# Segment sums of a Mamba stage: from full-height matmuls to differences of running sums on 32-row groups

## The chip, the cores and the metric

The kernel is one program on one core of a Trainium2 chip. The metric is the device time of one execution in microseconds (us). Three runs of the kernel before are shown, and one execution was profiled.

## The reference

A decoder trunk of two layers on 256 tokens of width 1024, in float32. Each layer adds to `h` first a combined mixer of three head groups (forgetting attention, HGRN2, Mamba-2), then cross-attention to 256 memory tokens, then a SwiGLU (layer 0) or a top-2-of-8 mixture of experts (layer 1). The part that matters here is the Mamba-2 group, 8 heads in 2 groups:

```python
a_dt = dt * a                       # one value per token and head, never positive
a_cum = jnp.cumsum(a_dt, axis=-1)
seg = a_cum[..., :, None] - a_cum[..., None, :]
lmat = masked_exp(seg, _causal_mask(ln))
cb = jnp.einsum('bclgn,bcsgn->bgcls', cc, bc)
y_diag = jnp.einsum('bgecls,bcsgep->bclgep', cb[:, :, None] * lmat, xc)
...
y = (y_diag + y_off) + d_skip * xs
```

`seg` for tokens l and s is the sum of `a_dt` over the tokens after s and up to l. The kernel takes the whole sequence as two tiles of 128 tokens, so each head has three blocks of 128 x 128: tile 0 to itself, tile 0 to tile 1, tile 1 to itself.

## The kernel before

Five engines run their own instruction streams, written out by hand, and meet by semaphores. Weights come in chunks of up to 1 MB (SyncE's queue, a ring of 4 slots, `RING`). Of each chunk ScalarE makes a "high" part (`whi`, L594, a ring of 3, `HRING`) and VectorE the remainder, the "low" (`wlo`, L1556). TensorE multiplies high by high, high by low and low by high (L1039 to L1041). `split_to(n)` makes highs or lows up to chunk n, `after(name)` up to three chunks past the projection `name`. A chunk takes TensorE 48 matmuls of 256 columns or 24 of 512.

Projections are interleaved with the heads' work, in this order in each layer: gates, `hq_hf`, `fq_fk`, `fv_hi`, the forgetting attention, `xbc0`, `xbc1` (inputs of the Mamba convolution), nine levels of the HGRN2 heads (L1180, L1185; 64-row matmuls of two alternating row groups) with `z` between them, then `xk0`, and the Mamba stage:

1. half of `xk0`, the outputs of the HGRN2 heads (L1198 to L1200, PSUM bank 7), the other half of `xk0`;
2. the products of B and C (L1208, L1209) and the transposes of x (L1212), in banks 4 to 7. ScalarE copies the transposes to `xs` (L802), VectorE masks the products into `CBs` (L1854);
3. round 0, heads 0 to 3: the segment sums in banks 4 to 7. ScalarE takes their exponential into `Mm` (L806), VectorE multiplies by `CBs` (L1872);
4. half of `xk1`, then round 1, heads 4 to 7, in the same banks, then the other half of `xk1`;
5. the heads' products with x (L1233 to L1235), which wait for both products of `Mm` (`m2_m`) and signal `m2_y`.

A round makes three full-height fp32 matmuls for each head. `ALm` holds the token's value at every column below it, and `ABm` the value at all columns (VectorE expands both ahead of the stage, L1841 and L1843):

```python
nc.tensor.matmul(b[:, 0:2 * P], ALm[:, 0, hd, :], upto_ones, start=True, stop=False)
nc.tensor.matmul(b[:, P:2 * P], ABm[:, hd, :], upto, start=False, stop=True)
mm = nc.tensor.matmul(b[:, 2 * P:3 * P], ALm[:, 1, hd, :], upto, start=True, stop=True)
```

Round 0 waits for `m2_a` (the expansions), `m2_cb` (L1854) and `m2_xs` (L802).

Of the kernel before, what the change touches and what calls it, by code (L numbers as in the profile page):

```python
# [38 lines left out]
EPS = 1e-6  # L39
FLOOR = 1e-30  # L40
# [49 lines left out]
for _name, _w in (("ident", P), ("minus_half", 20), ("neg", P), ("upto", P), ("ones", P), ("after", P), ("m2mask", 3 * P),  # L90
                  ("before", P), ("restart", 2 * S), ("iota", P), ("pair", NE)):
    CCOL[_name] = (_n, _n + _w)
    _n += _w
# [3 lines left out]
def constants():  # L97
# [4 lines left out]
    one = np.ones((P, P), np.float32)  # L102
    restart = np.broadcast_to((np.arange(2 * S) % 64 != 0).astype(np.float32), (P, 2 * S))
    parts = [np.eye(P, dtype=np.float32), np.full((P, 20), -0.5), (upto - np.eye(P)) * NEG, upto, one, (r[:, None] > r[None, :]) * 1.0,
             upto, one, upto, upto - np.eye(P), restart, np.broadcast_to(np.arange(P), (P, P)),
             (r[:, None] % NE == np.arange(NE)[None, :]) & (r[:, None] < 2 * NE)]
# [14 lines left out]
def build(nc, x, mem, par, con, lvl, lin_w, ffn_w, out):  # L121
# [31 lines left out]
    with ExitStack() as ctx:  # L153
# [86 lines left out]
        Mm = carve(8736, M2_H, 3 * P)  # L240
# [3 lines left out]
        ALm = carve(14368, NT, M2_H, P)  # L244
        ABm = carve(2560, M2_H, P)
# [124 lines left out]
        m2_a = sem("m2_a")  # L370
        m2_seg = sem("m2_seg")
        m2_e = sem("m2_e")
# [76 lines left out]
        def bank(name, layer):  # L449
            return 2 * (GI[name, layer] % 2)  # L450
# [5 lines left out]
        def _(sp):  # L456
# [125 lines left out]
        def _(act):  # L582
# [88 lines left out]
            for layer in range(DEPTH):  # L671
# [74 lines left out]
                ins.then_inc(fox_p, 1)  # L746
                def take_xbc(i):
# [48 lines left out]

                act.wait_ge(conv_ready, layer + 1)
                nc.scalar.activation(xcv, xcv, ACT.Silu).then_inc(xcv_ready, 1)
                take("z", layer, (zs, 0, 512, ACT.Silu, 1.0, None))
                split_to(last_chunk(layer, "xk0") + 2)  # L800
                act.wait_ge(m2_t, layer + 1)
                nc.scalar.activation(xs, pb[:, 6:8, :], ACT.Copy).then_inc(m2_xs, 1)  # L802
                take("xk0", layer, (tiles(kX[:, 0:4, :]), 0, 512, ACT.Copy, 1.0, None))
                for r in range(2):
                    act.wait_ge(m2_seg, 2 * layer + r + 1)
                    nc.scalar.activation(Mm[:, 4 * r:4 * r + 4, :], pb[:, 4:8, 0:3 * P], ACT.Exp).then_inc(m2_e, 1)  # L806
                    if r == 1:
                        split_to(chunk0(layer, "xk1") + HRING)
# [195 lines left out]
        def _(pe):  # L1004
# [96 lines left out]
            for layer in range(DEPTH):  # L1101
# [50 lines left out]
                project("xbc1", layer, X, (0,))  # L1152
                pe.wait_ge(fox_ptc, layer + 1)
# [37 lines left out]
                project("xk0", layer, M, (0,))  # L1191
                pe.wait_ge(hg_sel, (layer + 1) * (MASKED + 1))
                pe.wait_ge(hg_wide, (layer + 1) * len(WIDE))
                for hd in range(HG_H):
                    v = vtok[:, :, 256 + hd * DH:256 + (hd + 1) * DH]
                    at = 4 * (hd % 2) + 2 * (hd // 2)
                    o = pb[:, 7, :].rearrange("p (t h d) -> p t h d", t=NT, h=HG_H)
# [7 lines left out]
                pe.wait_ge(hg_ok, layer + 1)  # L1205
# [8 lines left out]
                pe.wait_ge(m2_a, layer + 1)  # L1214
                pe.wait_ge(m2_cb, layer + 1)
                pe.wait_ge(m2_xs, layer + 1)
                for rnd in range(2):
                    if rnd:
                        project("xk1", layer, M, (0,))
                        pe.wait_ge(m2_e, 2 * layer + 1)  # L1220
                    for i in range(4):
                        hd = 4 * rnd + i
                        b = pb[:, 4 + i, :]
                        nc.tensor.matmul(b[:, 0:2 * P], ALm[:, 0, hd, :], upto_ones, start=True, stop=False)  # L1224
                        nc.tensor.matmul(b[:, P:2 * P], ABm[:, hd, :], upto, start=False, stop=True)  # L1225
                        mm = nc.tensor.matmul(b[:, 2 * P:3 * P], ALm[:, 1, hd, :], upto, start=True, stop=True)  # L1226
                    mm.then_inc(m2_seg, 1)
                project("xk1", layer, M, (1,))
                pe.wait_ge(m2_m, 2 * layer + 2)
                for hd in range(M2_H):  # L1230
                    xh = xcd[:, :, hd * DH:(hd + 1) * DH]
                    o = slice(hd * DH, (hd + 1) * DH)
                    nc.tensor.matmul(pb[:, 4, o], Mm[:, hd, 0:P], xh[:, 0, :], start=True, stop=True)  # L1233
                    nc.tensor.matmul(pb[:, 5, o], Mm[:, hd, P:2 * P], xh[:, 0, :], start=True, stop=False)  # L1234
                    mm = nc.tensor.matmul(pb[:, 5, o], Mm[:, hd, 2 * P:3 * P], xh[:, 1, :], start=False, stop=True)  # L1235
# [303 lines left out]
        def _(dve):  # L1539
# [119 lines left out]
            for layer in range(DEPTH):  # L1659
# [120 lines left out]
                V.tensor_reduce(nmax[:, 4:8], pb[:, 4:8, P:3 * P], AX.X, ALU.max, negate=True).then_inc(fox_max, 1)  # L1780
                after("fv_hi", layer)
# [482 lines left out]
```

## Time and profile before

| | |
|---|---|
| time, median of 3 runs | 1516.91 us (1515.53 to 1518.87) |
| the profiled execution: time | 1518.24 us |
| the profiled execution: span from first to last instruction | 1515.9 us |
| mean granted TensorE clock | 0.995 of full |
| TensorE, VectorE, ScalarE busy | 1481.3, 1174.5, 940.8 us |
| Mamba stage in the span | about 117 to 154 us (layer 0) and 563 to 599 us (layer 1) |

In a timeline the first number is the start in us from the begin of the span, the second the length. A matmul's length holds its way through the array, and successive ones overlap: what one costs is the distance to the next start. An fp32 matmul leaves two records (x2), one of fp32r or a transpose one. The number in brackets at the end is the engine's idle time before the row, and behind the arrow the instruction that ended it.

### The profile page before, as it was taken

What the parts mean: (1) busy time and instruction counts of PE and PEld (TensorE: products, weight loads), DVE (VectorE), ACT (ScalarE), POOL (GpSimd) and SP (SyncE); (2) the same over time, 40 slices, a digit from 0 to 9 for tenths busy, and PEclk for the clock granted to TensorE, in tenths of its full rate; (3) what the DMA queues carried; (4) which work ended last, traced back from release to release, by engine and by line L of the source; (5) the groups of instructions that cost most, each with busy time, mean ns of one, the idle gap of its engine ahead of it and who ended that gap; (6) DMA issues with size and microseconds to landing.
All of it is one profiled execution on the core that took longest, in us unless ns stands there. A gap on an engine that the chain in (4) does not pass through costs nothing.

```text
span 1515.9 us, 21517 instructions
## 1 busy us (share of the span) xinstructions
PE 1481.3 (98%) x8411; PEld 1288.7 (85%) x8411; DVE 1174.5 (77%) x1140; ACT 940.8 (62%) x959; POOL 52.2 (3%) x58
## 2 busy tenths in 40 slices
PE   8999999999999999999999999999999999999996
PEld 7989898999889989897788888888888888888885
DVE  6886655555437886646998988989989899898995
ACT  6645344444337653454677778777787777777774
POOL 0031000000000031000000000000000000000000
PEclk9999999999999999999999999999999999999998
DMA  8433443454546432544699999999999998999993
GB/s 308 142 136 103 150 165 127 151 191 174 191 153 228 148 113 84 194 140 167 228 360 383 347 353 356 351 377 359 343 358 348 378 363 339 362 354 373 362 362 128
DMA packets 54478, 388.41 MB, mean 256 GB/s; under 512 B 6000, under 2 KB 6256, under 8 KB 8176
## 3 DMA queue, kind: packets, MB, share of 16 engines
q1 hardware_dynamic: 53840, 384.98, 67.8%
q10 hardware_dynamic: 544, 2.10, 0.4%
q8 instruction: 69, 1.13, 0.3%
q14 instruction: 25, 0.20, 0.0%
HBM read 386.00 MB, written 1.05 MB: 255 GB/s over the span
## 4 chain that ended last, share of the span: by engine, by line
issue 53%; PE 44%; DVE 2%; DMA 0%; ACT 0%; POOL 0%; POOLq 0%; DVEq 0%
PE pb L1039 12%; PE pb L1041 12%; PE pb L1040 12%; PE pb L1180 1%; PE pb L1258 1%; PE pb L1278 1%; PE pb L1020 1%; DVE xTl L1605 0%; PE pb L1224 0%; DMA h<-in_x 0%; PE pb L1268 0%; PE pb L1235 0%; PE pb L1226 0%; PE pb L1234 0%; PE pb L1225 0%
## 5 line engine op out<-in xcount | busy, mean ns | idle before, releaser
L2121 DVE TENSOR_TENSOR wlo<-raw,whi 128x2048 fp32r<-128x2048 f32 x175 | 400.3, 2291 | 47.7 <-ACT whi L941 45.9
L941 ACT ACTIVATE whi<-raw 128x2048 fp32r<-128x2048 f32 x175 | 335.6, 1920 | 132.0 <-PE pb L1041 132.0
L1556 DVE TENSOR_TENSOR wlo<-raw,whi 128x2048 fp32r<-128x2048 f32 (+1 forms) x101 | 225.7, 2246 | 133.2 <-ACT whi L594 132.7
L1039 PE MATMUL pb<-whi,mTh 128*128 128x512 f32 x768 | 305.2, 397 | 1.6 <-DVE wlo L2121 1.6
L1041 PE MATMUL pb<-whi,mTl 128*128 128x512 f32 x768 | 300.1, 391 | 0.0
L594 ACT ACTIVATE whi<-raw 128x2048 fp32r<-128x2048 f32 (+1 forms) x101 | 189.9, 1884 | 176.9 <-PE pb L1041 166.2
L1039 PE MATMUL pb<-xTh,whi 128*128 128x256 f32 x736 | 210.2, 286 | 2.0 <-DVE xTl L1593 1.2
L2121 DVE TENSOR_TENSOR kvXr<-kvX,whi 128x2048 fp32r<-128x2048 f32 x86 | 196.7, 2291 | 19.3 <-ACT whi L941 17.8
L1040 PE MATMUL pb<-xTl,whi 128*128 128x256 f32 x736 | 208.2, 283 | 0.0
L1041 PE MATMUL pb<-xTh,wlo 128*128 128x256 f32 x736 | 208.2, 283 | 0.0
L1040 PE MATMUL pb<-wlo,mTh 128*128 128x512 f32 x528 | 205.6, 389 | 0.0
L941 ACT ACTIVATE whi<-kvX 128x2048 fp32r<-128x2048 f32 x86 | 165.2, 1920 | 57.7 <-PE pb L1041 57.5
L1039 PEld LDWEIGHTS pb<-whi,mTh 128*128 128x128 f32 x768 | 144.2, 188 | 31.1 <-DVE wlo L2121 2.9
L1041 PEld LDWEIGHTS pb<-whi,mTl 128*128 128x128 f32 x768 | 144.1, 188 | 31.1
L1039 PEld LDWEIGHTS pb<-xTh,whi 128*128 128x128 f32 x736 | 141.1, 192 | 3.7 <-issue 2.1
L1040 PEld LDWEIGHTS pb<-xTl,whi 128*128 128x128 f32 x736 | 141.2, 192 | 0.1
L1041 PEld LDWEIGHTS pb<-xTh,wlo 128*128 128x128 f32 x736 | 141.1, 192 | 0.0
L1039 PE MATMUL pb<-whi,xhTh 128*128 128x512 f32 x352 | 138.5, 393 | 0.3 <-DVE wlo L2121 0.3
L1041 PE MATMUL pb<-whi,xhTl 128*128 128x512 f32 x352 | 137.1, 390 | 0.0
L1040 PEld LDWEIGHTS pb<-wlo,mTh 128*128 128x128 f32 x528 | 99.3, 188 | 19.8
L1040 PE MATMUL pb<-kvXr,mTh 128*128 128x512 f32 x240 | 93.5, 389 | 0.0
L1040 PE MATMUL pb<-wlo,xhTh 128*128 128x512 f32 x240 | 93.4, 389 | 0.0
(334 smaller groups left out, 2223.2 us busy)
## 6 DMA issues: line engine op xcount, KB each, us to landing
raw<-in_ffn_w SPq DMA_DIRECT2D x209, 1024.0 KB, 4.8
kvX<-in_ffn_w SPq DMA_DIRECT2D x88, 1024.0 KB, 4.9
raw<-in_lin_w SPq DMA_DIRECT2D x64, 1024.0 KB, 4.8
raw<-in_lin_w SPq DMA_DIRECT2D x4, 536.0 KB, 5.6
arena<-in_mem ACTq DMA_DIRECT2D x2, 1024.0 KB, 8.2
h<-in_x SPq DMA_DIRECT2D x1, 1024.0 KB, 5.0
out<-xn SPq DMA_DIRECT2D x2, 512.0 KB, 3.1
consts<-in_con SPq DMA_DIRECT2D x1, 836.0 KB, 14.0
```

The lines of the kernel that those rows point to most:

```text
L594: nc.scalar.activation(whi[:, m % HRING, c], raw[:, m % RING, c], ACT.Copy).then_inc(hi_ready, 1)
L941: nc.scalar.activation(whi[:, (MOE0 + c) % HRING, :], xraw_slots[c % XRING], ACT.Copy).then_inc(hi_ready, 1)
L1020: mm = nc.tensor.transpose(pb[:, turn_bank(no, b), i * S + t * P:i * S + (t + 1) * P], xn[:, t, k * P:(k + 1) * P], ident)
L1039: nc.tensor.matmul(o, lh, rh, start=first, stop=False)
L1040: nc.tensor.matmul(o, lh, rl, start=False, stop=False)
L1041: return nc.tensor.matmul(o, ll, rh, start=False, stop=last)
L1180: mm = nc.tensor.matmul(pb[:, b + hd % 2, i * P:(i + 1) * P], K[r, o + t * P:o + (t + 1) * P], Q[r, o + t * P:o + (t + 1) * P], start=True ...
L1258: mm = nc.tensor.matmul(pb[:, 4 + hd, t * S:(t + 1) * S], qX[:, 2 * hd + k, t * P:(t + 1) * P], kX[:, 2 * hd + k, :], start=(k == 0), stop ...
L1278: mm = nc.tensor.matmul(pb[:, 4 + hd, k * S:(k + 1) * S], vX[:, m, c:c + P], PTx[:, hd, m, :], start=(m == 0), stop=(m == 1))
L1556: V.tensor_tensor(wlo[:, m % RING, c], raw[:, m % RING, c], whi[:, m % HRING, c].bitcast(F32), ALU.subtract).then_inc(lo_ready, 1)
L2121: V.tensor_tensor(xlo_slots[c % XRING], xraw_slots[c % XRING], whi[:, (MOE0 + c) % HRING, :].bitcast(F32), ALU.subtract).then_inc(lo_ready, 1)
```

## The change

The segment sums are made as differences of running sums.

- In the forgetting-attention stage VectorE makes for each head and tile a value rounded to a coarse step (`COARSE`) and the rest, in four columns of each 32-column group of `Wm`. Four matmuls of TensorE, for both rounds, give their running sums over the tokens in bank 7 (`m2_c`), four rows for each of four heads of a round, on rows 0, 32, 64 and 96. ScalarE scales and shifts them by a table of 0, 1 and -1 (`units`) into `Qm` and `Km` (`m2_rows`), ahead of its work for `xbc0`.
- A round is then eight matmuls on 32 rows each: for i = 0 to 3, rows 32i to 32i+31, one of 256 columns into bank 4+i, and then four of 128 columns.
- Since rounded differences can come out above zero, VectorE takes the minimum with 0 of the two blocks of a tile with itself, in place in PSUM (`nonpositive`), before ScalarE's exponential.
- Round 0 moves ahead of the outputs of the HGRN2 heads, which go to the second bank of `z` and wait for `z`'s evacuation. Round 1 moves behind the first half of `xk1`. `Mm` becomes two tiles.
- ScalarE evacuates `z` ahead of `xcv`, takes exponential 0 ahead of `xk0`, then `xk0`, `xs`, exponential 1.
- VectorE: the expansions go; squares of the heads ahead of `CBs`; product 0 and `xcd` ahead of the low that `after("xk0")` makes; `ytmp` and the low of `xk1`'s ring behind the heads' normalisation.
- SyncE requests the level masks (`lmask`, 512 KB, first used by the HGRN2 levels) behind chunk 7 instead of chunk 3 of layer 0.

```diff
@@ SyncE
                     load(chunk0(layer, PROJ[0][0]) + c, lin_w[layer * LIN_CHUNKS + c])
+                    if layer == 0 and c == RING + 3:
+                        sp.dma_start(lmask[:, :, :].rearrange("p a b -> p (a b)"), lvl).then_inc(masks_in, 16)
                     if layer == 0 and c == RING - 1:
                         sp.dma_start(consts[:, early:], con[:, early:]).then_inc(tables_in, 16)
                         sp.dma_start(params[:, columns:], par[:, columns:]).then_inc(tables_in, 16)
-                        sp.dma_start(lmask[:, :, :].rearrange("p a b -> p (a b)"), lvl).then_inc(masks_in, 16)
@@ ScalarE, behind the attention's exponentials
+                act.wait_ge(m2_c, layer + 1)
+                units = [const("units")[:, i:i + 1] for i in range(4)]
+                sums = pb[:, 7, :].rearrange("p (r s) -> p r s", r=2)
+                nc.scalar.activation(Qm, sums, ACT.Identity, scale=units[0], bias=units[1])
+                nc.scalar.activation(Km, sums, ACT.Identity, scale=units[2], bias=units[3]).then_inc(m2_rows, 1)
@@ ScalarE, the stage
+                projected(act, "z", layer)
+                b = bank("z", layer)
+                nc.scalar.activation(zs, pb[:, b:b + 2, 0:512], ACT.Silu).then_inc(lin_act, 1)
                 act.wait_ge(conv_ready, layer + 1)
                 nc.scalar.activation(xcv, xcv, ACT.Silu).then_inc(xcv_ready, 1)
-                take("z", layer, (zs, 0, 512, ACT.Silu, 1.0, None))
-                split_to(last_chunk(layer, "xk0") + 2)
+                after("z", layer)
+                def decays(r):
+                    act.wait_ge(m2_neg, 2 * layer + r + 1)
+                    nc.scalar.activation(Mm[r], pb[:, 4:8, 0:3 * P], ACT.Exp).then_inc(m2_e, 1)
+                decays(0)
+                take("xk0", layer, (tiles(kX[:, 0:4, :]), 0, 512, ACT.Copy, 1.0, None))
                 act.wait_ge(m2_t, layer + 1)
                 nc.scalar.activation(xs, pb[:, 6:8, :], ACT.Copy).then_inc(m2_xs, 1)
-                take("xk0", layer, (tiles(kX[:, 0:4, :]), 0, 512, ACT.Copy, 1.0, None))
-                for r in range(2):
-                    act.wait_ge(m2_seg, 2 * layer + r + 1)
-                    nc.scalar.activation(Mm[:, 4 * r:4 * r + 4, :], pb[:, 4:8, 0:3 * P], ACT.Exp).then_inc(m2_e, 1)
-                    if r == 1:
-                        split_to(chunk0(layer, "xk1") + HRING)
+                decays(1)
+                split_to(chunk0(layer, "xk1") + HRING)
@@ TensorE, behind the transposes of the attention weights
+                pe.wait_ge(m2_w, layer + 1)
+                for rnd in range(2):
+                    o = pb[:, 7, rnd * S:(rnd + 1) * S]
+                    nc.tensor.matmul(o[:, 0:P], Wm[:, 0, rnd, :], const("after"), start=True, stop=True)
+                    mm = nc.tensor.matmul(o[:, P:S], Wm[:, 1, rnd, :], upto, start=True, stop=True)
+                mm.then_inc(m2_c, 1)
@@ TensorE, the stage
                 project("xk0", layer, M, (0,))
+                def segments(rnd):
+                    for i in range(4):
+                        r = slice(32 * i, 32 * i + 32)
+                        nc.tensor.matmul(pb[:, 4 + i, 0:2 * P], Km[r, rnd, 0:P], Qm[r, rnd, :], start=True, stop=True)
+                    for i in range(4):
+                        r = slice(32 * i, 32 * i + 32)
+                        mm = nc.tensor.matmul(pb[:, 4 + i, 2 * P:3 * P], Km[r, rnd, P:S], Qm[r, rnd, P:S], start=True,
+                                              stop=True)
+                    mm.then_inc(m2_seg, 1)
                 pe.wait_ge(hg_sel, (layer + 1) * (MASKED + 1))
                 pe.wait_ge(hg_wide, (layer + 1) * len(WIDE))
+                segments(0)
+                pe.wait_ge(lin_act, evac_count(("z", layer)))
...
                 mm.then_inc(m2_t, 1)
-                pe.wait_ge(m2_a, layer + 1)
+                project("xk1", layer, M, (0,))
                 pe.wait_ge(m2_cb, layer + 1)
                 pe.wait_ge(m2_xs, layer + 1)
-                for rnd in range(2):
...
+                segments(1)
+                pe.wait_ge(hg_ok, layer + 1)
                 project("xk1", layer, M, (1,))
                 pe.wait_ge(m2_m, 2 * layer + 2)
@@ VectorE, behind the maxima of the attention
+                for t in range(NT):
+                    ins = V.tensor_scalar(Z12[:, t, 4:12], A12[:, t, 4:12], 2.0 * t - 1.0, COARSE, ALU.mult, ALU.add)
+                link(ins)
+                for t in range(NT):
+                    at = Wm[:, t, :, :].rearrange("p r (i x) -> p r i x", x=32)
+                    V.tensor_scalar(at[:, :, :, 0:2], pairs(Z12[:, t, 4:12]), -COARSE, None, ALU.add)
+                    ins = V.scalar_tensor_tensor(out=at[:, :, :, 2:4], in0=pairs(Z12[:, t, 4:12]), scalar=-COARSE,
+                                                 in1=pairs(A12[:, t, 4:12]), op0=ALU.add,
+                                                 op1=ALU.subtract if t else ALU.add)
+                ins.then_inc(m2_w, 1)
@@ VectorE, the stage
-                V.tensor_copy(ABm, bc(A12[:, 1, 4:12], P))
-                for t in range(NT):
-                    ins = V.tensor_tensor(ALm[:, t, :, :], const("after").unsqueeze(1).to_broadcast([P, M2_H, P]),
-                                          bc(A12[:, t, 4:12], P), ALU.mult)
-                ins.then_inc(m2_a, 1)
+                def nonpositive(rnd):
+                    dve.wait_ge(m2_seg, 2 * layer + rnd + 1)
+                    own = pb[:, 4:8, 0:3 * P].rearrange("p b (i s) -> p b i s", i=3)[:, :, 0:3:2, :]
+                    V.tensor_scalar(own, own, 0.0, None, ALU.min).then_inc(m2_neg, 1)
+                nonpositive(0)
...
+                split_to(last_chunk(layer, "xk0") + 2)
                 dve.wait_ge(m2_t, layer + 1)
                 V.tensor_tensor(CBs, pb[:, 4:6, 0:3 * P], const("m2mask")...
+                decayed(0)
+                dve.wait_ge(m2_xs, layer + 1)
+                for t in range(NT):
+                    V.tensor_tensor(by_heads(xcd, t), by_heads(xs, t), bc(SP12[:, t, 4:12], DH), ALU.mult)
                 after("xk0", layer)
+                nonpositive(1)
+                decayed(1)
                 root()
```

## Rows read from the trace of the kernel before

**Rows 1.** The page: busy time by engine, and the chain that ended last, by engine.

```profile
PE 1481.3 (98%) x8411; PEld 1288.7 (85%) x8411; DVE 1174.5 (77%) x1140; ACT 940.8 (62%) x959; POOL 52.2 (3%) x58
...
issue 53%; PE 44%; DVE 2%; DMA 0%; ACT 0%; POOL 0%; POOLq 0%; DVEq 0%
```

**Rows 2.** TensorE's timeline, layer 0: start, length, line, operation, count, idle before.

```profile
117.61 0.33 PE L1198 MATMUL pb<-arena 128*128 128x64 f32 x2
...
129.59 0.67 PE L1224 MATMUL pb<-consts,arena 128*128 128x256 f32 x2 [1.21 <-ACT arena L802]
...
130.54 0.60 PE L1224 MATMUL pb<-consts,arena 128*128 128x256 f32 x2
130.98 0.38 PE L1225 MATMUL pb<-consts,arena 128*128 128x128 f32 x2
131.20 0.39 PE L1226 MATMUL pb<-consts,arena 128*128 128x128 f32 x2
...
133.10 0.36 PE L1039 MATMUL pb<-mTh,whi 128*128 128x256 f32 x1
...
138.92 0.59 PE L1224 MATMUL pb<-consts,arena 128*128 128x256 f32 x2
...
142.21 0.39 PE L1226 MATMUL pb<-consts,arena 128*128 128x128 f32 x2
142.35 0.36 PE L1039 MATMUL pb<-mTh,whi 128*128 128x256 f32 x1
...
148.18 0.33 PE L1233 MATMUL pb<-arena 128*128 128x64 f32 x2
```

**Rows 3.** TensorE's timeline, the same stage in layer 1.

```profile
575.13 0.67 PE L1224 MATMUL pb<-consts,arena 128*128 128x256 f32 x2 [1.21 <-ACT arena L802]
...
593.72 0.33 PE L1233 MATMUL pb<-arena 128*128 128x64 f32 x2
```

**Rows 4.** TensorE's timeline, the first two levels of the second heads, layer 0.

```profile
88.11 2.16 PE L1180 MATMUL pb<-arena 64*128 64x128 f32 x32
90.19 0.50 PE L1039 MATMUL pb<-whi,xTh 128*128 128x512 f32 x1
90.53 0.39 PE L1040 MATMUL pb<-wlo,xTh 128*128 128x512 f32 x1
90.76 0.39 PE L1041 MATMUL pb<-whi,xTl 128*128 128x512 f32 x1
```

**Rows 5.** ScalarE's timeline, layer 0.

```profile
90.09 1.07 ACT L751 ACTIVATE arena<-pb 128x512 f32<-128x512 f32 x2
...
113.59 1.28 ACT L798 ACT_TABLE_LOAD   x1
...
142.63 1.46 ACT L806 ACTIVATE arena<-pb 128x1536 f32<-128x1536 f32 x1 [7.71 <-PE pb L1226]
```

**Rows 6.** VectorE's timeline, layer 0.

```profile
28.51 2.23 DVE L1556 TENSOR_TENSOR wlo<-raw,whi 128x2048 fp32r<-128x2048 f32 x1
...
68.27 1.76 DVE L1789 COPY arena<-pb 128x1536 f32<-128x1536 f32 x1 [0.92 <-PE pb L1147]
...
70.17 2.29 DVE L1556 TENSOR_TENSOR wlo<-raw,whi 128x2048 fp32r<-128x2048 f32 x1
...
128.43 0.96 DVE L1854 TENSOR_TENSOR arena<-pb,consts 128x768 f32<-128x768 f32 x1 [5.10 <-PE pb L1212]
...
144.12 1.76 DVE L1872 TENSOR_TENSOR arena<-arena 128x1536 f32<-128x1536 f32 x1 [3.66 <-ACT arena L806]
...
153.68 1.22 DVE L1885 TENSOR_TENSOR xn<-arena,pb 128x1024 f32<-128x1024 f32 x1 [3.53 <-PE pb L1235]
```

**Rows 7.** TensorE's timeline around its first weight wait, layer 0.

```profile
30.58 0.28 PE L1041 MATMUL pb<-xTh,wlo 128*128 128x256 f32 x1
30.89 0.35 PE L1039 MATMUL pb<-xTh,whi 128*128 128x256 f32 x1
```

**Rows 8.** Line L1224: weight loads, length in ns (lowest, median, highest).

```profile
L1224 PEld LDWEIGHTS pb<-consts,arena x32: 186/192/192, 129.6 to 587.1; 128*128 128x128 f32 x32
```

More of the change, by code:

```diff
@@ L39 @@
 EPS = 1e-6
+COARSE = 3.0 * 2.0 ** 10
 FLOOR = 1e-30
@@ L90 @@
 for _name, _w in (("ident", P), ("minus_half", 20), ("neg", P), ("upto", P), ("ones", P), ("after", P), ("m2mask", 3 * P),
-                  ("before", P), ("restart", 2 * S), ("iota", P), ("pair", NE)):
+                  ("before", P), ("restart", 2 * S), ("iota", P), ("pair", NE), ("units", 4)):
     CCOL[_name] = (_n, _n + _w)
@@ L102, in constants @@
     one = np.ones((P, P), np.float32)
+    row = [(np.arange(P)[:, None] % 32 == i) * 1.0 for i in range(4)]
     restart = np.broadcast_to((np.arange(2 * S) % 64 != 0).astype(np.float32), (P, 2 * S))
@@ L243, in build @@
         xcd = carve(4608, NT, 512)
-        ALm = carve(14368, NT, M2_H, P)
-        ABm = carve(2560, M2_H, P)
+        Wm = carve(9760, NT, 2, P)
+        Km = carve(2560, 2, S)
+        Qm = carve(3072, 2, S)
         ytmp = carve(3584, NT, 512)
@@ L1152, in _ @@
                 project("xbc1", layer, X, (0,))
+                pe.wait_ge(m2_rows, layer + 1)
                 pe.wait_ge(fox_ptc, layer + 1)
@@ L1852, in _ @@
                 after("z", layer)
-                dve.wait_ge(m2_t, layer + 1)
-                V.tensor_tensor(CBs, pb[:, 4:6, 0:3 * P], const("m2mask").unsqueeze(1).to_broadcast([P, 2, 3 * P]),
-                                ALU.mult).then_inc(m2_cb, 1)
-                after("xk0", layer)
-                dve.wait_ge(m2_xs, layer + 1)
-                for t in range(NT):
-                    tokens = xs[:, t, :].rearrange("p (h d) -> p h d", d=DH)
-                    V.tensor_tensor(xcd[:, t, :].rearrange("p (h d) -> p h d", d=DH), tokens, bc(SP12[:, t, 4:12], DH),
-                                    ALU.mult)
-                    V.tensor_tensor(ytmp[:, t, :].rearrange("p (h d) -> p h d", d=DH), tokens,
-                                    bc(par_("m2_d", layer), DH), ALU.mult)
                 dve.wait_ge(hg_ok, layer + 1)
@@ L1867, in _, with by_heads, decayed @@
                 V.tensor_scalar(ss[:, :, 0:8], ss[:, :, 0:8], 1.0 / DH, EPS, ALU.mult, ALU.add).then_inc(ss_ready, 1)
-                dve.wait_ge(m2_cb, layer + 1)
-                for rnd in range(2):
-                    dve.wait_ge(m2_e, 2 * layer + rnd + 1)
-                    m = Mm[:, 4 * rnd:4 * rnd + 4, :]
-                    V.tensor_tensor(m, m, CBs[:, rnd, :].unsqueeze(1).to_broadcast([P, 4, 3 * P]),
-                                    ALU.mult).then_inc(m2_m, 1)
-                split_to(chunk0(layer, "xk1") + HRING)
+                def by_heads(ap, t):
+                    return ap[:, t, :].rearrange("p (h d) -> p h d", d=DH)
+                def decayed(rnd):
+                    dve.wait_ge(m2_e, 2 * layer + rnd + 1)
+                    V.tensor_tensor(Mm[rnd], Mm[rnd], CBs[:, rnd, :].unsqueeze(1).to_broadcast([P, 4, 3 * P]),
+                                    ALU.mult).then_inc(m2_m, 1)
+                split_to(last_chunk(layer, "xk0") + 2)
+                dve.wait_ge(m2_t, layer + 1)
+                V.tensor_tensor(CBs, pb[:, 4:6, 0:3 * P], const("m2mask").unsqueeze(1).to_broadcast([P, 2, 3 * P]),
+                                ALU.mult).then_inc(m2_cb, 1)
+                dve.wait_ge(m2_cb, layer + 1)
+                decayed(0)
+                dve.wait_ge(m2_xs, layer + 1)
+                for t in range(NT):
+                    V.tensor_tensor(by_heads(xcd, t), by_heads(xs, t), bc(SP12[:, t, 4:12], DH), ALU.mult)
+                after("xk0", layer)
+                nonpositive(1)
+                decayed(1)
                 root()
@@ L1881, in _ @@
                 V.tensor_tensor(xn[:, :, 256:512], xn[:, :, 256:512], gate, ALU.mult).then_inc(xn_ready, 1)
+                for t in range(NT):
+                    ins = V.tensor_tensor(by_heads(ytmp, t), by_heads(xs, t), bc(par_("m2_d", layer), DH), ALU.mult)
+                link(ins)
+                split_to(chunk0(layer, "xk1") + HRING)
                 dve.wait_ge(m2_y, layer + 1)
```

37 lines of the change are left out of this document (17 added, 20 removed).

## The prediction

> **What bounds the kernel now.** I read the page first: TensorE is busy for 98% of the span, the other engines for 77% or less, and the chain that ended last is matmuls of TensorE and their issue for 97% [rows 1]. So only two things can change the time: what TensorE has to issue in the Mamba stage, and its waits there. All that follows is in a fixed order, and the experts' loads start behind a semaphore of the attention after the stage (`xa_o`). What the stage wins is therefore won at the end of the kernel too.
>
> Next TensorE's timeline of the stage in layer 0 [rows 2]. Three things are to be seen. After the products of B and C and the transposes TensorE stands idle for 1.21 us, until ScalarE has copied `xs` (L802). Then come the segment sums of round 0, from 129.59 to 133.10, 3.51 us, and, behind half of `xk1`, those of round 1, from 138.92 to 142.35, 3.43 us. Last, the other half of `xk1` takes 5.83 us (142.35 to 148.18) with no idle time ahead of the heads' first matmul (L1233), though round 1's exponentials and products are made meanwhile. Layer 1 repeats it: 1.21 us idle, and 18.59 us from there to L1233 (575.13 to 593.72) as in layer 0 (129.59 to 148.18) [rows 2, 3]. So 3.51 + 3.43 + 1.21 = 8.15 us of each layer are at stake, 16.3 us in all.
>
> **The change, part by part.**
>
> Removed from TensorE: both rounds as they are, and, since `xk1`'s first half now stands ahead of the waits for `m2_cb` and `m2_xs`, the idle time. -8.15 us per layer.
>
> Added in the forgetting-attention stage: four fp32 matmuls of 128 columns and all 128 rows (running sums for two rounds). That form stands 0.22 us from its successor (L1225 at 130.98, L1226 at 131.20 [rows 2]). 4 x 0.22 = +0.9 us per layer, all on the path.
>
> The new rounds: four matmuls of 256 columns and four of 128, on 32 rows each, successive ones on different groups of 32. No row shows 32-row matmuls, so the price is bounded.
> - One after the other: 0.44 us for 256 columns (L1224, 130.54 to 130.98), 0.22 for 128, so 4 x 0.44 + 4 x 0.22 = 2.64 us a round.
> - The only packed rows are those of the levels, 64 rows in two groups: 16 matmuls of 128 columns in 2.08 us (88.11 to 90.19) [rows 4]. That is 0.13 each instead of 0.22, a factor of 0.59; by it a round takes 2.64 x 0.59 = 1.56 us.
> - Four groups wholly side by side: 0.44 + 0.22 = 0.66 us, and a loss like that of the levels over their ideal (16 x 0.22 / 2 = 1.76 against 2.08, 0.32 for two levels; I take 0.25): 0.9 us.
> I take 1.2 us, halfway between the last two: four groups should beat two, but the matmuls are issued in order. Two rounds: +2.4 us.
>
> Going back from packed to full-height matmuls costs something in the rows: 0.34 us from the first to the second (90.19 to 90.53), where the next pair is 0.23 apart [rows 4]. The Trainium skill (TensorEngine Tiling (Array Packing), Key Properties) says that changing the tiling mode drains TensorE, which speaks against two separate packed rounds in each layer. By that rule each of the four visits costs about what the row shows, 0.1 us at its end, and the trace agrees in that.
>
> Sum: 8.15 - 0.9 - 2.4 = 4.85 us per layer, 9.7 us in all.
>
> **What I cost at nothing, and its cover** (times on the clock of before; all of it comes 0.9 us later).
> - ScalarE now waits for the running sums ahead of the high of `xbc1`'s second chunk, whose low VectorE made at 70.17. The transposes are through at 68.27 [rows 6], the sums' matmuls at 69.2, two PSUM copies of 512 columns (1.07 the pair, [rows 5]) at 70.3, the high (1.9) at 72.2, the low (2.29) at 74.5. TensorE wants it one chunk (5.8 us) ahead of the levels, at 88.11 - 5.8 = 82.3. VectorE's six small instructions (at most 0.2 us each) lie ahead of a wait for TensorE (0.92 us at 68.27).
> - The second heads' output moves to a bank of `z` and waits for `z`'s evacuation. ScalarE does that first now, behind the table load at 113.59 (1.28): done at 115.9 [rows 5]. TensorE gets there at 117.61 + 1.2 = 118.8. 2.9 us of cover.
> - Round 0: the min (1.22 us, by the 1024-column row L1885 with its PSUM operand [rows 6]), the table load and the Exp (1.46) are done by 122.5. What overwrites these banks, the products of B and C, stands at 127.3.
> - Round 1 is narrow. `xk1`'s first half ends at 135.3, the round at p = 136.5. From there: 0.28 us until the last matmul is out, min 1.22, Exp 1.46, product 1.76, and 0.25 for four hand-overs (0.03 us from L1226's end at 142.60 to ScalarE at 142.63 [rows 2, 5]; I allow 0.1 where VectorE hands over): 4.97 us, under 5.83 us of `xk1`. 0.86 us are left. VectorE must be free for the min at 136.8: CBs (0.96) from 129.6, product of round 0 to 132.3, two of `xcd` (0.7 each for 512 columns, estimated from CBs' 0.96 for 768) to 133.7, the low of `xv0`'s first chunk to 136.0. 0.8 us are left.
> - VectorE loses the three expansions into ALm and ABm and gains two mins and the small ones; `ytmp` and the next low end at 147.3, before `m2_y` at 147.8.
> - The masks' request (512 KB) goes behind chunk 7. The one gap that it could close is TensorE's before 30.89, 0.31 instead of 0.12 us [rows 7]. The low that ends it begins at 28.51 right behind VectorE's fills (L1697) [rows 6], so it is VectorE that is late there, not the load. I take 0; the other end is a gain of 0.2 us. From its new place, some 50 us ahead of the first selection, nothing waits for it.
>
> If round 1's cover were gone, every microsecond over 0.86 would cost one per layer; a min of twice the length costs 0.36 per layer.
>
> **The numbers.** The profiled execution took 1518.24 us (its span and 2.34 around it), and should take 1508.5. The median of the runs is 1.33 us lower, 1516.91; less 9.7 it is 1507.2.
>
> **Rivals.**
> - Four groups side by side: 0.9 us a round, 8.15 - 0.9 - 1.8 = 5.45 a layer, 10.9 in all: 1506.0. For it: the levels lose only 0.32 us over an ideal overlap. Against it: the passes are issued in order, and both of one matmul come before the next group's. The Trainium skill (TensorE: Matmul & The Clock Gate, Part 3) gives 3.07 times for four 32-row matmuls of 512 columns; an estimate by that page is 2.64 / 3.07 = 0.86 us a round and 1505.9.
> - The factor of the levels, 1.56 us: 4.13 a layer, 8.3 in all: 1508.6.
> - The change doesn't do what it says, and the groups run one after the other: 2.64 us, 1.97 a layer: 1513.0. Against it: the levels' rows.
> - A new wait takes the place of the idle time: VectorE is late for the second min, or the min is long. 0.5 to 1.5 us a layer: 1508.2 to 1510.2. For it: two margins under 1 us. Against it: nothing else stands in the two queues there.
> - Loads are hidden, but each matmul's whole length shows: 0.60 and 0.38 us (L1224, L1225 [rows 2]), 3.9 a round, 8.15 - 0.9 - 7.8 = -0.55 a layer: 1518.0, no difference.
> - Slower: a change of row group hides neither. A pass then costs its weight load, 0.19 us [rows 8], and its own record, 0.39 for 256 columns and 0.27 for 128 (0.60 and 0.38 less one spacing): 8 x 0.58 + 8 x 0.46 = 8.3 us a round, +9.3 a layer: 1535.6. From 4.4 us a round on, (8.15 - 0.9 + 1.5) / 2, it makes the kernel slower by over 0.2%. Against it: the levels change groups throughout, at 0.13 us a matmul.
>
> **How the numbers follow.** Forecast 0.40, four side by side 0.22, the levels' factor 0.16, one after the other 0.07, a new wait 0.07, whole lengths 0.04, nothing hidden 0.04. The range, 1504.5 to 1511.0, holds the first three and most of the new waits, with 1.5 us or more around the two bounds of a round for the spread of the runs (1515.53 to 1518.87 before), and leaves out some 0.17. 0.2% (3.0 us) is about what a measurement of this kernel can tell from no change: faster 0.92, within it 0.04, slower 0.04.
>
> **What would show it.** In the profile after: no idle time of TensorE for `xs`; packed rounds of eight matmuls in 0.9 to 1.6 us; four matmuls of 128 columns behind the transposes of the attention weights; round 1's product done before `xk1` ends; the heads' first matmul near 143.3 (148.18 - 4.85) and 584.0 (593.72 - 9.7). The prediction is wrong if a round takes over 2 us, if TensorE waits for the product of round 1, or if another stage loses what this one wins.

## The result, and the profile after

The changed kernel takes 1506.19 us (median of 4 runs, 1505.31 to 1506.49), against 1517.32 us (4 runs, 1515.53 to 1518.87) for the kernel before: a ratio of 0.9926, 95% interval 0.9909 to 0.9943. It is 11.1 us faster; forecast were 9.7, and 10.9 by the rival "four groups side by side". The interval, 8.6 to 13.8 us, holds both, so the times alone don't tell them apart; the profile does. The profiled execution took 1506.49 us with a span of 1504.1 us, 11.8 below that of before.

The page after, its part 1 and the chain by engine, is to be held against [rows 1]. TensorE is busy for 8.3 us less and is still the bound.

```profile
PE 1473.0 (98%) x8395; PEld 1280.7 (85%) x8395; DVE 1175.0 (78%) x1150; ACT 943.5 (63%) x963; POOL 53.4 (4%) x58
...
issue 53%; PE 43%; DVE 2%; DMA 1%; ACT 0%; POOL 0%; POOLq 0%; SPq 0%; DVEq 0%
```

TensorE's timeline after, layer 0 and then the last two groups of rows from layer 1; it answers to [rows 2, 3].

```profile
67.27 1.53 PE L1167 MATMUL pb<-consts,arena 128*128 128x128 f32 x12
68.64 0.39 PE L1173 MATMUL pb<-consts,arena 128*128 128x128 f32 x2
...
69.31 0.39 PE L1174 MATMUL pb<-consts,arena 128*128 128x128 f32 x2
69.45 0.36 PE L1059 MATMUL pb<-xTh,whi 128*128 128x256 f32 x1
...
118.94 0.28 PE L1061 MATMUL pb<-mTh,wlo 128*128 128x256 f32 x1
119.15 0.71 PE L1223 MATMUL pb<-arena 32*128 32x256 f32 x8
119.68 0.40 PE L1226 MATMUL pb<-arena 32*128 32x128 f32 x8
120.01 0.43 PE L1238 MATMUL pb<-arena 128*128 128x64 f32 x2
120.28 0.39 PE L1239 MATMUL pb<-arena 128*128 128x64 f32 x2
...
129.86 1.04 PE L1252 MATMUL pb<-consts,arena 128*128 128x128 f32 x8
130.65 0.36 PE L1059 MATMUL pb<-mTh,whi 128*128 128x256 f32 x1
...
136.57 0.71 PE L1223 MATMUL pb<-arena 32*128 32x256 f32 x8
137.11 0.40 PE L1226 MATMUL pb<-arena 32*128 32x128 f32 x8
137.44 0.39 PE L1059 MATMUL pb<-mTh,whi 128*128 128x256 f32 x1
...
143.30 0.33 PE L1264 MATMUL pb<-arena 128*128 128x64 f32 x2
...
576.57 0.71 PE L1223 MATMUL pb<-arena 32*128 32x256 f32 x8
577.11 0.40 PE L1226 MATMUL pb<-arena 32*128 32x128 f32 x8
577.44 0.39 PE L1059 MATMUL pb<-mTh,whi 128*128 128x256 f32 x1
...
583.30 0.33 PE L1264 MATMUL pb<-arena 128*128 128x64 f32 x2
```

Four things are to be seen. The running sums stand in 0.81 us (68.64 to 69.45); from the transposes' first row to the projection's it is 2.18 us (67.27 to 69.45) instead of 1.29 (66.70 to 67.99 before), so they cost 0.89. Between the transposes of x (L1252) and `xk1` no idle time is left. A packed round takes 0.87 us from its first start to the next projection's (136.57 to 137.44, and the same in layer 1; round 0 takes 0.86, 119.15 to 120.01), where a round took 3.43 to 3.51. And `xk1` runs straight into the heads' products, at 143.30 instead of 148.18 and at 583.30 instead of 593.72.

Where the 11.8 us of the two profiled executions lie is read from distances on TensorE's timeline, which an earlier shift doesn't touch:

| from, to | before | after | difference |
|---|---|---|---|
| start of the span to the transposes of the attention weights, layer 0 | 66.70 | 67.27 | +0.57 |
| these transposes to the Mamba heads' first product, layer 0 | 81.48 | 76.03 | -5.45 |
| the same, layer 1 | 80.18 | 74.63 | -5.55 |
| heads' first product to cross-attention's first, layers 0 and 1 | 70.64; 70.62 | 70.64; 70.64 | 0.0 |
| the router's transposed sums to the first wait of the experts (layer 1) | 20.72 | 19.30 | -1.42 |

The two differences of the stage are the rival's 5.45 us within 0.1. The last line isn't the change's: before, TensorE's granted clock was low (0.53 from 722.4 to 726) while the tokens were gathered, which stretches the records there. After, the low stretch (0.63 from 705.6 to 709.6) falls mostly on the idle-filling matmuls ahead of the ranks, and the waits that stand at other times behind the filling (0.49 and 0.99 us) are gone, so it costs nothing. Repeated executions of one and the same kernel differ by such stretches of 1.3 to 1.5 us (see the first experiment).

### The profile page after: what moved, and what is told of

It is laid out like the page before. It is cut to its first block, busy times and chain, and to the rows that moved or that the text cites. A ratio compares the mean times of both kernels' runs of the same rounds, so it can differ in the third digit from the quotient of the medians.

```text
span 1504.1 us, 21505 instructions
## 1 busy us (share of the span) xinstructions
PE 1473.0 (98%) x8395; PEld 1280.7 (85%) x8395; DVE 1175.0 (78%) x1150; ACT 943.5 (63%) x963; POOL 53.4 (4%) x58
## 3 DMA queue, kind: packets, MB, share of 16 engines
HBM read 386.00 MB, written 1.05 MB: 257 GB/s over the span
## 4 chain that ended last, share of the span: by engine, by line
issue 53%; PE 43%; DVE 2%; DMA 1%; ACT 0%; POOL 0%; POOLq 0%; SPq 0%; DVEq 0%
PE pb L1059 12%; PE pb L1061 12%; PE pb L1060 12%; PE pb L1207 1%; PE pb L1289 1%; PE pb L1309 1%; DMA arena<-in_mem 1%; PE pb L1040 1%; DMA raw<-in_lin_w 0%; DVE xTl L1636 0%; DVE wlo L1587 0%; PE pb L1299 0%; PE pb L1266 0%; PE pb L1265 0%; PE pb L1158 0%
```

## The experiments

**The changed kernel again**, unedited.

> The changed kernel once more, as the standard for the others on this chip. Theory (the stage gives 5.45 us a layer, less 0.57 us lost at the start of layer 0): 1504 to 1507 us, with heads' first matmul of layer 0 near 143.3. The rest of the profiled difference, 1.4 us in the expert routing, came from where TensorE's granted clock was at its lower level (0.53 from 722.4 to 726 before, 0.63 from 705.6 to 709.6 after). If that place wanders between executions, this profile may show it elsewhere, and the time then moves by up to 1.5 us with nothing changed. Rival: the low stretch belongs to the change and falls in the same place again.

Measured: 1505.15 us (5 runs, 1505.06 to 1506.49), ratio 0.992 [0.9907, 0.9933] to 1517.31 (23 runs). The stage takes 74.75 and 74.63 us in the two layers. Its time in the routing is 20.72 us, not 19.30, though the kernel is the same. In turn its third wide level has its usual length. The first of these rows is TensorE's timeline of the kernel after, the second that of the repetition:

```profile
109.07 3.77 PE L1207 MATMUL pb<-arena 64*128 64x128 f32 x32 [0.59 <-DVE arena L1858]
```

```profile
108.99 2.16 PE L1207 MATMUL pb<-arena 64*128 64x128 f32 x32 [0.60 <-DVE arena L1858]
```

What follows: a stretch of low clock falls now here, now there, and costs some 1.3 to 1.5 us each time (76.03 against 74.75 for the stage in layer 0 is this one). The kernel before had it too, in the same place: its 81.48 us in layer 0 are 80.08 in the same kernel with only the masks' request moved (below). So differences of about 1.5 us between two single profiles say nothing here, and the stage alone gives the change's size: 80.08 or 80.18 less 74.75 or 74.63, 5.3 to 5.55 us a layer.

**The masks' request back behind chunk 3.**

```diff
-                    if layer == 0 and c == RING + 3:
-                        sp.dma_start(lmask[:, :, :].rearrange("p a b -> p (a b)"), lvl).then_inc(masks_in, 16)
                     if layer == 0 and c == RING - 1:
...
+                        sp.dma_start(lmask[:, :, :].rearrange("p a b -> p (a b)"), lvl).then_inc(masks_in, 16)
```

> The changed kernel with the level masks' request back behind chunk 3. Theory: the late request is what brought the memory tokens 0.56 us later (23.17 instead of 22.61), since chunk 4's load now runs beside theirs; that idle time of VectorE became TensorE's 0.41 us before 31.45. Undone, VectorE starts at 22.6 again, TensorE's gap falls back to 0.31 between starts, and the heads' first matmul comes 0.4 to 0.6 us earlier: 142.8. Rival: the memory load's time varies by itself, and the start doesn't change. In the time it is 0.5 us, under what the rounds can tell; the profile decides.

Measured: 1506.32 us (6 runs, 1504.77 to 1510.12), ratio 0.9932 [0.992, 0.9945]; stage 74.65 and 74.75 us. By the median that is 1.2 us more than the repetition and not less; the ranges overlap.

**The masks' later request alone**, in the kernel before (the opposite edit).

> The kernel before with nothing but the masks' request moved behind chunk 7. Theory: the first 105 us are lengthened by 0.4 to 0.6 us (the memory tokens land near 23.2, the first level wait of TensorE near 106.3 instead of 105.75), the stage is as before: 1517.5 to 1518 by the median of before. Rival (what the prediction had): 0 to 0.2 us gained.

Measured: 1516.31 us (11 runs, 1515.42 to 1519.10), ratio 0.9996 [0.9988, 1.0005], no difference that can be told, and not the expected 1517.5 to 1518; stage 80.08 and 80.19 us, as before. The place that the move could touch is TensorE's first wait for weights, [rows 7]. Here are its rows in the kernel after (masks late), and then in the one with the masks early:

```profile
30.77 0.28 PE L1061 MATMUL pb<-xTh,wlo 128*128 128x256 f32 x1
31.45 0.36 PE L1059 MATMUL pb<-xTh,whi 128*128 128x256 f32 x1 [0.41 <-DVE wlo L1587]
```

```profile
30.66 0.28 PE L1060 MATMUL pb<-xTh,wlo 128*128 128x256 f32 x1
31.17 0.36 PE L1058 MATMUL pb<-xTh,whi 128*128 128x256 f32 x1 [0.23 <-DVE wlo L1586]
```

What follows: these rows look like a loss. The distance is 0.31 (before) and 0.51 us with the masks early, 0.68 (after) and 0.72 (masks late alone) with the masks late. But the other profiles don't bear it out. In the unedited repetition of the changed kernel, whose masks are late too, it is 0.20 us (31.16 to 31.36). Over all profiles it runs from 0.12, which is no gap, to 0.51 us in the three kernels with the request early, and from 0.12 to 1.27 in the nine with it late. The memory tokens, with which ScalarE begins, land at 22.61 to 22.91 us in the three and at 22.46 to 23.60 in the nine: the ranges overlap. So do the starts of the attention weights' transposes, 66.70 to 67.30 and 66.64 to 67.71, and the times can't tell. It stays open whether the move costs a few tenths of a us or nothing; no run shows that it wins something.

**Full height.** The rounds as three full-height matmuls a head, as before, but from the two-part operands and in the new order. Each head's exponents are then summed over all 128 rows, that is over four heads, so the decays are others; the work is the same in size.

```diff
                     for i in range(4):
-                        r = slice(32 * i, 32 * i + 32)
-                        nc.tensor.matmul(pb[:, 4 + i, 0:2 * P], Km[r, rnd, 0:P], Qm[r, rnd, :], start=True, stop=True)
-                    for i in range(4):
-                        r = slice(32 * i, 32 * i + 32)
-                        mm = nc.tensor.matmul(pb[:, 4 + i, 2 * P:3 * P], Km[r, rnd, P:S], Qm[r, rnd, P:S], start=True,
+                        nc.tensor.matmul(pb[:, 4 + i, 0:2 * P], Km[:, rnd, 0:P], Qm[:, rnd, :], start=True, stop=False)
+                        nc.tensor.matmul(pb[:, 4 + i, P:2 * P], Km[:, rnd, 0:P], Qm[:, rnd, P:S], start=False, stop=True)
+                        mm = nc.tensor.matmul(pb[:, 4 + i, 2 * P:3 * P], Km[:, rnd, P:S], Qm[:, rnd, P:S], start=True,
```

> The changed kernel, but the segment sums of a round are made by the shapes of before: for each head one matmul of 256 columns and two of 128 over all 128 rows (they add up the four heads, so the decays are not the reference's). The new order, the minima and the running sums stay. Theory: the packing is worth 3.45 - 0.87 = 2.6 us a round, 10.3 us in all, and the order only the idle time of 1.21 less the running sums' 0.9, so nearly nothing: this kernel takes 1516 to 1517 us. Rival: the order gives more than the idle time, and half of the gain stays (near 1511).

Measured: 1515.65 us (10 runs, 1514.79 to 1518.00), ratio 0.9992 [0.9983, 1.0001]; stage 79.63 us in layer 0 and 80.96 in layer 1, where the third wide level was stretched (3.56 instead of 2.16 us). The time is just under the expected 1516 to 1517. In its timeline a round is again 3.5 us, from 117.60 to 121.11:

```profile
117.60 0.60 PE L1222 MATMUL pb<-arena 128*128 128x256 f32 x2
...
120.89 0.39 PE L1224 MATMUL pb<-arena 128*128 128x128 f32 x2
121.11 0.33 PE L1236 MATMUL pb<-arena 128*128 128x64 f32 x2
```

What follows: the order alone (no idle time for `xs`, running sums added) is worth 80.08 less 79.63, 0.45 us a layer, where the forecast's terms make 1.21 less 0.9, 0.3. The packing is worth the rest, 79.63 less 74.75, 4.9 us a layer, some nine tenths of the whole.

**One group.** All matmuls of a round on rows 0 to 31. They compute the first head's decays for all four heads; the count and the size of the matmuls are those of the changed kernel.

```diff
-                        r = slice(32 * i, 32 * i + 32)
+                        r = slice(0, 32)
```

(in both loops of a round)

> The changed kernel with all eight matmuls of a round on rows 0 to 31, so that nothing can run side by side (every head of a round gets the decays of its first head, not the reference's). Theory: it is the four row groups that make a round short; without them it takes 4 x 0.44 + 4 x 0.22 = 2.64 us instead of 0.87, 1.77 us more in each of four rounds, 7.1 us in all, near 1512.3. Rival: a 32-row matmul is itself shorter than a full-height one, whatever its group, and the time stays near 1505.5 to 1508.

Measured: 1520.54 us (10 runs, 1517.45 to 1523.74), ratio 1.0023 [1.0014, 1.0033]. TensorE's timeline of round 0, layer 0:

```profile
117.83 1.99 PE L1223 MATMUL pb<-arena 32*128 32x256 f32 x8
119.66 1.05 PE L1226 MATMUL pb<-arena 32*128 32x128 f32 x8
120.64 0.43 PE L1238 MATMUL pb<-arena 128*128 128x64 f32 x2
```

A round takes 2.81 us (117.83 to 120.64), 1.94 more than the packed one, so four cost 7.8 us. That settles what makes the round short: not that a matmul has few rows, but that successive ones lie in different groups. Without it the forecast's "one after the other" (2.64 us) is about right. The time is 15 us above the changed kernel's 1505.15, though, not 8, and outside both expectations. In the profiled execution (1519.04 us) the two stages take 80.05 and 81.79 us, 12.5 more than in the repetition of the changed kernel (74.75 and 74.63); 7.8 of that are the rounds, and the other 4.7 are clock. The median run is another 1.5 us longer, which no profile shows. Windows of this kernel and then of the changed one; the number behind the POOL column is the granted clock:

```profile
122.00:130.00 8.00, 8.00 (x56) 8.00 (x56) 5.83 (x6) 3.25 (x2) 0.33 (x1) 0.79 0.00 1
130.00:140.00 10.00, 10.00 (x78) 9.61 (x77) 7.91 (x6) 3.74 (x3) 4.55 (x1) 1.00 0.37 115
...
556.00:570.00 14.00, 13.95 (x105) 13.16 (x101) 4.90 (x5) 12.65 (x11) 0.00 (x0) 0.88 0.22 76
570.00:580.00 10.00, 10.00 (x71) 9.90 (x70) 7.61 (x6) 2.65 (x3) 3.20 (x1) 0.83 0.10 21
```

```profile
122.00:130.00 8.00, 8.00 (x67) 7.90 (x66) 6.99 (x6) 4.94 (x4) 1.49 (x1) 1.00 0.25 81
130.00:140.00 10.00, 10.00 (x94) 9.72 (x92) 7.98 (x7) 3.71 (x4) 3.40 (x1) 1.00 0.48 170
```

Both low stretches lie behind round 0 (117.83 in layer 0, 563.34 in layer 1). Behind round 1 the clock stays at 1.00 (142 to 150 and 588 to 600).

**The min of round 1 three times**, which makes the chain behind the round 2.5 us longer and changes no value.

```diff
+                    if rnd:
+                        link(V.tensor_scalar(own, own, 0.0, None, ALU.min))
+                        link(V.tensor_scalar(own, own, 0.0, None, ALU.min))
```

> The changed kernel with round 1's minimum done three times over, each linked to the one before (the result is the same). Theory: the chain from round 1 to the heads' matmuls has its own cover. By the prediction it was 0.86 us; by the profile after, the product ends at 142.09 and the heads begin at 143.30, 1.2 us. Two further minima are 2.5 us, so TensorE waits 1.3 to 1.7 us ahead of the heads in each layer, and the kernel takes 2.6 to 3.4 us more: 1508 to 1509. Rival: VectorE has more room than the chain shows, and nothing moves.

Measured: 1513.57 us (9 runs, 1512.55 to 1519.41), ratio 0.9982 [0.9973, 0.9992]. VectorE's timeline and then TensorE's, layer 0:

```profile
136.74 1.23 DVE L1891 TENSOR_SCALAR pb<-pb 128x1024 f32<-128x1024 f32 x1 [0.48 <-PE pb L1226]
138.01 1.23 DVE L1892 TENSOR_SCALAR pb<-pb 128x1024 f32<-128x1024 f32 x1
139.28 1.23 DVE L1893 TENSOR_SCALAR pb<-pb 128x1024 f32<-128x1024 f32 x1
142.03 1.76 DVE L1915 TENSOR_TENSOR arena<-arena 128x1536 f32<-128x1536 f32 x1 [1.52 <-ACT arena L821]
```

```profile
143.84 0.43 PE L1264 MATMUL pb<-arena 128*128 128x64 f32 x2 [1.22 <-DVE arena L1915]
```

Two more mins are 2.54 us (136.74 to 139.28), TensorE waits for 1.22 of them in each layer, so the changed kernel has 1.32 us of cover left. Against 1505.15 the time rose by 8.4 us, where the two waits make 2.4 and the forecast for this run was 2.6 to 3.4 (in the profiled execution, the longest of the nine, the span rose by 13.0). The heads' stretch up to cross-attention took 75.65 and 75.63 us instead of 70.64, in windows of this clock:

```profile
136.00:144.00 8.00, 6.78 (x65) 6.44 (x62) 5.93 (x6) 3.46 (x3) 0.00 (x0) 1.00 0.45 141
144.00:150.00 6.00, 6.00 (x37) 6.00 (x37) 5.18 (x6) 2.51 (x2) 0.00 (x0) 0.64 0.41 164
150.00:156.00 6.00, 6.00 (x26) 5.62 (x26) 3.17 (x3) 1.68 (x4) 0.00 (x0) 0.51 0.00 0
```

**The same, with the wait filled**: nine matmuls of the identity between `xk1` and the wait, into a bank that nobody reads. They compute nothing that is used.

```diff
+                pe.wait_ge(m2_e, 2 * layer + 2)
+                for i in range(9):
+                    nc.tensor.matmul(pb[:, 6, 0:P], ident, ident, start=True, stop=True)
                 pe.wait_ge(m2_m, 2 * layer + 2)
```

> The min of round 1 stands three times, as before, and nine matmuls of the identity (128 columns, full height, into a bank that nobody reads; 16 of them took 2.05 us in the routing, so about 1.15 us) stand between xk1 and TensorE's wait of 1.22 us ahead of the heads' products; they compute nothing that is used. Theory A (the idle time itself starts the stretch at the lower clock): the heads' products still start 1.4 us late in each layer (76.1 us from the transposes), but the stretch from there to cross-attention comes back from 75.6 to 70.6 us, and the time is 1507.5 to 1509, some 5 below the kernel with the bare wait. Theory B (the clock falls for another reason in these kernels, as the late start of the heads against the other engines): the stretch stays at 75.6 us and the time at 1512 to 1515.

Measured: 1509.17 us (4 runs, 1508.45 to 1510.67), ratio 0.9946 [0.9929, 0.9962]. Its TensorE timeline, and its windows behind that:

```profile
142.19 2.17 PE L1262 MATMUL pb<-consts 128*128 128x128 f32 x18
144.19 0.33 PE L1267 MATMUL pb<-arena 128*128 128x64 f32 x2
```

```profile
144.00:150.00 6.00, 6.00 (x57) 6.00 (x56) 5.20 (x7) 2.23 (x2) 0.00 (x0) 1.00 0.39 157
150.00:156.00 6.00, 6.00 (x30) 5.01 (x29) 5.86 (x9) 1.57 (x4) 1.01 (x1) 1.00 0.00 0
```

The nine take 2.0 us and not 1.15: the row with 16 records was eight matmuls, two records each. So the heads start 2.0 us late in each layer, 0.8 more than they must. Still the kernel is faster than with the bare wait (1514.78 us on the same chip, below), because the stretch to cross-attention is back at 70.69 and 70.68 us with the clock at full. Theory A's stretch and time came out. It says no more than that filling this wait removes the fall: the kernel before waited as long, 1.21 us [rows 2], without one.

**The bare wait again**, on the chip of the filled one.

> The kernel with the min of round 1 three times and the bare wait, once more, on the chip of the filled one. Both theories: a wait of 1.22 us ahead of the heads in each layer, 1512.5 to 1515.5 us. If it shows no low granted clock behind the wait and is near 1508, the loss of 5 us a layer was of that one execution.

Measured: 1514.78 us (10 runs, 1508.25 to 1517.93), ratio 0.9978 [0.996, 0.9996], and 1.22 us of wait in each layer again. The stretch took 74.00 and 75.63 us, with the clock at 0.64 and 0.54 in the windows 144 to 150 and 589 to 595. Three of its ten runs took 1508.25 to 1508.70, just what the two waits alone would make of 1506; the others 1512.45 to 1517.93. None of the nine runs of the first time was so short. The nineteen times lie near 1508.5, from 1512.5 to 1514.7 and from 1515.9 to 1519.4, as they would if the clock fell in neither, one or both layers; only two executions are profiled, and in them it fell in both. So the fall of the clock comes in most executions and not in all.

**VectorE's low ahead of the products that it could do first.**

```diff
+                after("xk0", layer)
...
-                after("xk0", layer)
```

> The changed kernel with VectorE's order at one place undone: the low of xv0's first chunk, which waits for its high (130.7), ahead of product 0 and xcd instead of behind them. Theory: VectorE comes to that place at 131.9 in the profile after, when the high is already there, so the same instructions run in another order with no wait between them, round 1's minimum starts when it did (137.6) and the time is that of the changed kernel. Rival: the order is what keeps the minimum in time, and TensorE waits ahead of the heads' matmuls, 1 to 2 us per layer.

Measured: 1505.90 us (4 runs, 1505.03 to 1506.80), ratio 0.9925 [0.991, 0.994]; stage 74.76 and 74.75 us. VectorE's timeline:

```profile
130.03 2.29 DVE L1587 TENSOR_TENSOR wlo<-raw,whi 128x2048 fp32r<-128x2048 f32 x1
132.24 1.75 DVE L1912 TENSOR_TENSOR arena<-arena 128x1536 f32<-128x1536 f32 x1
133.91 1.28 DVE L1924 TENSOR_TENSOR arena<-arena,small 128x512 f32<-128x512 f32 x2
135.68 1.23 DVE L1890 TENSOR_SCALAR pb<-pb 128x1024 f32<-128x1024 f32 x1 [0.49 <-PE pb L1226]
138.43 1.76 DVE L1912 TENSOR_TENSOR arena<-arena 128x1536 f32<-128x1536 f32 x1 [1.52 <-ACT arena L821]
```

The min still waits 0.49 us for the round (L1226), as in the changed kernel: in either order VectorE is free in time, and the order wins nothing.

**More filling in the routing**, with the masks early: the idle-filling matmuls ahead of the experts raised from 8 and 4 to 10 and 8.

```diff
-            keep_going(8)
+            keep_going(10)
...
-                    keep_going(4)
+                    keep_going(8)
```

> The changed kernel with the masks requested early and six more idle-filling matmuls of TensorE in the routing (10 instead of 8 ahead of the ranks, 8 instead of 4 ahead of the gather), 0.22 us each, where it stood idle for 0.49 and 0.99 us. Theory: the stretch at the lower clock level in the gather (0.53 from 722.4 to 726 in the kernel before, some 1.5 us lost) follows sparse work ahead of it; filled, the gather takes 13.4 us and not 15.0 from its first matmul to the experts' first wait in this profile, and the median is up to 1 us under that of the masks early alone. Rival: the low stretch comes whatever stands there, or the fill delays the ranks.

Measured: 1505.24 us (5 runs, 1505.03 to 1509.32), ratio 0.993 [0.9916, 0.9943]. The routing took 19.22 us without a stretch of low clock, but so did it in the kernel with the masks early alone, so these profiles don't test the filling. The median is 1.1 us under that kernel's 1506.32, as expected, but the ranges overlap widely (1505.03 to 1509.32 and 1504.77 to 1510.12), and against 1505.15 for the unedited kernel it is no gain that can be told. No version was measurably better than the changed kernel.

## Why the prediction was right, and what was off

1. **The removed 8.15 us a layer**: right. No idle time stands ahead of `xk1`, and 3.51 and 3.43 us of rounds are gone.
2. **The running sums**: right, 0.89 us for 0.9 (their rows alone, 0.81).
3. **The packed round is the term that was mis-sized**: 0.87 us, not 1.2. I had averaged the levels' factor (1.56) and the ideal with its loss (0.9), because the matmuls are issued in order. That order didn't keep four groups from taking their work almost wholly side by side, 0.87 us where the ideal was 0.66. Against the full-height price of 2.64 us that is a factor of 3.0, where the levels' two groups gave 1.7; against one group's measured 2.81 it is 3.2. By the page's factor (the Trainium skill, TensorE: Matmul & The Clock Gate, Part 3) a round was estimated at 0.86 us; the trace agrees, with 0.87. That factor is for matmuls of 512 columns; here it held for fp32 ones of 256 and 128.

   With rounds at 0.87 the forecast's sum is 8.15 - 0.89 - 1.74 = 5.52 a layer, and 5.3 to 5.55 were measured. Two more terms are in the rows and nearly cancel. The wait for `xs` cost more than its 1.21 us, since idle time is counted from the end of the last record, where a successor would have started earlier: from the transposes of x to the projection behind round 0 it was 5.75 us (127.35 to 133.10) and is 0.79 now (129.86 to 130.65), 4.96 less, where the forecast took 3.51 + 1.21 = 4.72. And a packed round costs more than its rows: round 0 lengthens the way from the projection to the second matmul of the HGRN2 outputs from 0.29 us (117.49 to 117.78) to 1.34 (118.94 to 120.28), so 1.05, and round 1 saves 2.48 (138.80 to 142.35 before, 136.37 to 137.44 after, 3.55 less 1.07). That makes 4.96 + 2.48 - 1.05 - 0.89 = 5.50.

   The prediction also read 0.1 us at the end of a packed stretch as the cost of going back to full height (0.34 instead of 0.23 us, [rows 4]), and held that for a sign of the drain. That reading was wrong. Behind full-height fp32 matmuls the first row of such a projection is 0.31 us from the next too (before, layer 0):

```profile
50.97 0.47 PE L1039 MATMUL pb<-whi,xTh 128*128 128x512 f32 x1
51.28 0.39 PE L1040 MATMUL pb<-wlo,xTh 128*128 128x512 f32 x1
```

   With 256 columns it is 0.20 us behind full-height ones (133.10 to 133.30) and 0.22 behind the packed round (137.44 to 137.66). So only 0.02 to 0.03 us of it are the packing's, and the rest comes with the change from fp32 matmuls to the projection's. What the rows show instead is the approach: 0.20 us from the projection to a packed round (136.37 to 136.57), where 0.12 is usual.

   The forecast's mechanism was right and its size low. Two hits are luck. The heads' first matmul, forecast near 143.3, came at 143.30, because layer 0 began 0.57 us late and won 0.6 more than forecast; the unedited repetition has it at 141.93. And 9.7 us is within the interval of the result, while the profile says 10.6 to 11.1.
4. **Cover costed at nothing**: right, no new wait stands in the stage. ScalarE's two copies with factors took 0.67 us each (69.73 to 70.41 to 71.08) instead of 0.53, and the low of `xbc1`'s second chunk ended at 75.4, not 74.5, with 82.3 as its limit. Behind round 1 the product ended at 142.09 against 143.30:

```profile
137.58 1.23 DVE L1890 TENSOR_SCALAR pb<-pb 128x1024 f32<-128x1024 f32 x1 [0.49 <-PE pb L1226]
140.33 1.76 DVE L1912 TENSOR_TENSOR arena<-arena 128x1536 f32<-128x1536 f32 x1 [1.52 <-ACT arena L821]
```

   The forecast's cover was 0.86 us, the measured one 1.32 by the tripled min, and 1.21 by these rows (143.30 less 142.09).
5. **What lies over that cover**: wrong, though nothing hung on it. I priced each microsecond at one per layer. The runs show 8.4 us (over 1505.15) and 8.6 us (over 1506.19) of time for 2.4 us of waits, since the clock falls behind them in most executions. If a wait of 0.5 to 1.5 us a layer does the same, which was run at 1.22 us only, the forecast's rival "a new wait", 1508.2 to 1510.2, was some 6 us too low.
6. **The masks**: 0 is not contradicted, and no gain was seen. The gap at 30.6 us is no measure of it: it varies from 0.20 to 0.68 us between two profiles of the changed kernel itself.
7. **The rest**: "one after the other" had the price right (2.64, measured 2.81 to the next row) for a case that the change isn't; whole lengths and "nothing hidden" fell with the first packed row.

## What to carry to other kernels

Here short matmuls of 32 rows paid only when successive ones lay in different row groups: eight of them on four groups took 0.87 us, on one group 2.81, at full height 3.5. Price such packing by the number of groups, and don't carry a factor over from two groups to four. And price a new wait of TensorE by more than its length: look at the granted clock behind it, and if it falls there and the wait can't be removed, try filling it with matmuls that compute nothing, even if these outlast it a little, as they did here by 0.8 us. And before calling a short distance in one profile an effect, look for it in a second profile of the same kernel.

## What the hardware showed that was not expected

- A wait of 1.22 us ahead of 48 records of 64 columns was followed by a granted clock near one half, the lower of its two levels, for most of the next 10 us (0.64, then 0.51), at a cost of 5.0 us in three of the four stretches profiled and 3.4 in the fourth; with the same matmuls behind a wait filled for 2.0 us it stayed at 1.00. In three of the nineteen timed runs of the bare wait the time shows no such loss. The kernel before waited for 1.21 us too [rows 2], with 3.5 us of full-height matmuls behind it, and its stretch to cross-attention took 70.64 us. That it is the kind of work behind the wait that decides was not tried.
- Round 0 on one row group, with no idle time, was also followed by low clock in both layers (0.79, 0.88, 0.83 in the windows shown), where round 0 on four groups was not. Round 1 on one row group was not followed by it. Behind round 0 stand fp32 matmuls of 64 columns, as behind the wait above, and behind round 1 the projection's of 256. Why was not tried.
